# Sums of squares of the forget projections: eight fp32 products against sixteen products of rounded parts made by VectorE

## The reference, cut to what matters

```python
h = rms_norm(x, mix_norm[i])
fq, fk, fv, f_logit, sq, sk, sv, g_fox, g_sb = split_columns(h @ w_in[i])
fq = rms_norm(fq.reshape(b, s_len, FOX_HEADS, HEAD_DIM), q_norm[i])
fk = rms_norm(fk.reshape(b, s_len, FOX_HEADS, HEAD_DIM), k_norm[i])
log_f = jax.nn.log_sigmoid((f_logit + forget_bias[i]).astype(jnp.float32))
y_fox = forgetting_attention(fq, fk, fv, log_f)   # uses F = jnp.cumsum(log_f, axis=1)
```

## Time and profile before

| what | value |
| --- | --- |
| median of 3 runs | 1674.89 us (1674.73 to 1675.24) |
| the profiled execution | 1675.06 us, span 1673.3 us |
| TensorE busy | 1667.3 us (100%), 7640 matmuls |
| VectorE busy | 1029.0 us (61%) |
| ScalarE busy | 638.6 us (38%) |
| GpSimd busy | 713.3 us (43%) |
| granted clock of TensorE | 1.00 |

### The profile page before, as it was taken

How to read it: one execution, slowest core, us unless ns; L and a number is a source line. 1 busy time by engine, 2 the same in 40 slices (tenths; PEclk the granted TensorE clock), 3 DMA queues, 4 the chain that set the end, 5 groups by cost and what they waited for, 6 DMA issues and landing times.

```text
span 1673.3 us, 21109 instructions
## 1 busy us (share of the span) xinstructions
PE 1667.3 (100%) x7640; PEld 1363.7 (81%) x7640; DVE 1029.0 (61%) x1237; ACT 638.6 (38%) x895; POOL 713.3 (43%) x303
## 2 busy tenths in 40 slices
PE   9999999999999999999999999999999999999999
PEld 7887888887788887888888888888778768888887
DVE  7767566526565458367665567776574753969451
ACT  5222222226665756321322322213446744333321
POOL 2444344434333431444444344434356533444443
PEclk9999999999999999999999999999999999999999
DMA  5332232325511320342433323332252033323343
GB/s 199 101 110 90 81 101 93 107 90 197 139 64 53 99 76 26 101 138 90 141 97 103 103 88 100 103 103 89 93 193 76 26 124 104 95 94 101 94 142 117
DMA packets 44192, 173.14 MB, mean 103 GB/s; under 512 B 5033, under 2 KB 5417, under 8 KB 42828
## 3 DMA queue, kind: packets, MB, share of 16 engines
q1 hardware_dynamic: 39024, 148.13, 27.2%
q10 hardware_dynamic: 5084, 23.82, 4.2%
HBM read 159.22 MB, written 10.62 MB: 101 GB/s over the span
## 4 chain that ended last, share of the span: by engine, by line
PE 96%; DVE 2%; ACT 1%; issue 0%; DMA 0%; POOL 0%; SPq 0%; DVEq 0%; ACTq 0%; POOLq 0%
PE psum L339 26%; PE psum L340 26%; PE psum L344 26%; PE psum L1297 1%; PE psum L331 1%; PE psum L333 1%; PE psum L332 1%; PE psum L363 1%; PE psum L366 1%; PE psum L399 1%; PE psum L1883 1%; PE psum L400 1%; PE psum L404 1%; PE psum L369 1%; PE psum L1860 1%; PE psum L1287 1%
## 5 line engine op out<-in xcount | busy, mean ns | idle before, releaser
L274 POOL TENSOR_TENSOR wlo<-raw,whi 128x1024 fp32r<-128x1024 f32 (+2 forms) x256 | 657.9, 2570 | 866.5 <-ACT whi L319 865.9
L319 ACT ACTIVATE whi<-raw 128x1024 fp32r<-128x1024 f32 (+2 forms) x259 | 286.1, 1105 | 699.8 <-PE psum L344 633.8
L339 PE MATMUL psum<-h_hi,whi 128*128 128x512 f32 x1304 | 515.1, 395 | 0.1
L340 PE MATMUL psum<-h_lo,whi 128*128 128x512 f32 x1304 | 507.9, 389 | 0.0
L344 PE MATMUL psum<-h_hi,wlo 128*128 128x512 f32 x1304 | 324.4, 389 | 0.0
L339 PEld LDWEIGHTS psum<-h_hi,whi 128*128 128x128 f32 x1304 | 244.9, 188 | 55.2 <-issue 4.9
L340 PEld LDWEIGHTS psum<-h_lo,whi 128*128 128x128 f32 x1304 | 244.9, 188 | 52.3 <-issue 2.6
L344 PEld LDWEIGHTS psum<-h_hi,wlo 128*128 128x128 f32 x1304 | 244.8, 188 | 50.9
L725 DVE TENSOR_TENSOR silu<-sig,gate 128x512 f32<-128x512 f32 x44 | 100.3, 2279 | 41.8 <-ACT sig L670 41.8
L339 PE MATMUL psum<-mid_hi,whi 128*128 128x512 f32 x308 | 120.1, 390 | 0.0
L340 PE MATMUL psum<-mid_lo,whi 128*128 128x512 f32 x308 | 119.8, 389 | 0.0
(11 more groups left out here) (423 smaller groups left out, 2504.6 us busy)
## 6 DMA issues: line engine op xcount, KB each, us to landing
raw<-wk_dram SPq DMA_DIRECT2D x220, 512.0 KB, 3.5
raw<-wd_dram SPq DMA_DIRECT2D x32, 704.0 KB, 4.1
raw<-wp_dram SPq DMA_DIRECT2D x8, 640.0 KB, 3.8
x_scratch<-xT ACTq DMA_DIRECT2D x2, 2048.0 KB, 8.5
spectra_scratch<-spec_out ACTq DMA_DIRECT2D x4, 1024.0 KB, 6.4
xT<-x_scratch ACTq DMA_DIRECT2D x8, 512.0 KB, 4.5
spec<-spectra_scratch ACTq DMA_DIRECT2D x2, 2048.0 KB, 10.3
xT<-x_dram SPq DMA_DIRECT2D x4, 512.0 KB, 7.5
```

The source lines that it names most:

```text
L274: pool.tensor_tensor(wlo[s][:, 0:w], raw[s][:, 0:w], whi[s][:, 0:w].bitcast(F32), ALU.subtract).then_inc(lo_ready, 1)
L319: act.activation(whi[s][:, 0:w], raw[s][:, 0:w], ACT.Copy).then_inc(hi_ready, 1)
L339: pe.matmul(dst, a, m_hi[:, c, :], start=start and c == chunks[0][0], stop=False)
L340: pe.matmul(dst, a, m_lo[:, c, :], start=False, stop=False)
```

## The change

Three things change in `FoxProjections`, and two carry them.

1. **Parts of the squares.** ScalarE still writes the square in plain float32. VectorE now makes a rounded part `head_sq_hi` (a cast, L1154 of the changed kernel) and the rest `head_sq_lo` (a subtraction, L1156). TensorE multiplies both parts by a float32r copy of the matrix, `block_ones_r` (L1039, L1040), and sum j waits for both parts. The parts of unit j + 1 are made ahead of the scaling of i = j, those of units 0 and 1 ahead of the first scaling.
2. **The scan.** `vector_sums` stands behind i = 7 and no longer behind i = 4.
3. **The last factor.** ScalarE computes the factor of unit 7 directly after that of unit 6, ahead of the high parts of unit 6.
4. `block_ones_r` takes the place of a mask that nothing used in the constants, and the rotary tables count on the semaphore `const_landed`. Neither changes the number of DMAs or their place.

```diff
             def tensor_square_sum(self, pe, i):
-                pe.wait_ge(self.sq, i + 1)
+                pe.wait_ge(self.sq_parts, 2 * i + 2)
                 if i >= 2:
                     pe.wait_ge(self.std, i - 1)
-                pe.matmul(bank(4 + i % 2), block_ones, head_sq[i % 2][:, :], start=True, stop=True).then_inc(self.sum, 1)
+                pe.matmul(bank(4 + i % 2), block_ones_r, head_sq_hi[i % 2][:, :], start=True, stop=False)
+                pe.matmul(bank(4 + i % 2), block_ones_r, head_sq_lo[i % 2][:, :], start=False,
+                          stop=True).then_inc(self.sum, 1)
...
                         if j >= 2:
-                            act.wait_ge(self.sum, j - 1)
+                            act.wait_ge(self.sq_parts, 2 * j - 2)
                         act.activation(head_sq[j % 2][:, :], self.bank(j), ACT.Square).then_inc(self.sq, 1)
...
+                    if 0 < j < 8:
+                        i = j - 1
+                        self.scalar_factor(act, i)
+                        if j == 7:
+                            self.scalar_factor(act, 7)
...
+                self.vector_square_parts(dve, 0)
                 for i in range(8):
+                    if i + 1 < 8:
+                        self.vector_square_parts(dve, i + 1)
                     dve.wait_ge(self.rstd, i + 1)
...
                         self.vector_steps(dve)
-                    elif i == 4:
+                    elif i == 7:
                         self.vector_sums(dve)
...
+            def vector_square_parts(self, dve, j):
+                hi, lo = head_sq_hi[j % 2], head_sq_lo[j % 2]
+                dve.wait_ge(self.sq, j + 1)
+                if j >= 2:
+                    dve.wait_ge(self.sum, j - 1)
+                dve.tensor_copy(hi[:, :], head_sq[j % 2][:, :]).then_inc(self.sq_parts, 1)
+                dve.wait_ge(self.sq_parts, 2 * j + 1)
+                dve.tensor_tensor(lo[:, :], head_sq[j % 2][:, :], hi[:, :].bitcast(F32),
+                                  ALU.subtract).then_inc(self.sq_parts, 1)
```

More of the change, by code:

```diff
@@ L125, in build @@
         ident, block_ones, ones, before = (constf[:, i, :] for i in range(4))
-        ident_r, neg_tri, neg_ones, mask_qk, mask_kq = (constr[:, i, :] for i in range(5))
+        ident_r, neg_tri, neg_ones, mask_qk, block_ones_r = (constr[:, i, :] for i in range(5))
         head_sq = [square, sumsq]
@@ L160, in build @@
         forgets = at(100, "forgets", [P, T], F32R)
+        head_sq_hi = [at(88 + 2 * i, f"head_sq_hi{i}", [P, T], F32R) for i in range(2)]
+        head_sq_lo = [at(92 + 2 * i, f"head_sq_lo{i}", [P, T], F32R) for i in range(2)]
         probT = [at(104 + 2 * i, f"probT{i}", [P, T]) for i in range(2)]
@@ L413, in build @@
         const_landed = sem("const_landed")
-        rope_landed = sem("rope_landed")
         constr_ready = sem("constr_ready")
@@ L991, in __init__ @@
                 (self.sq, self.sum, self.std, self.rstd, self.f32, self.hi, self.ready, self.cleared, self.forget,
-                 self.softplus, self.v) = (
+                 self.softplus, self.v, self.sq_parts) = (
                     sem(f"fox_{x}") for x in ("square", "head_sum", "std", "rstd", "f32", "hi", "qk_ready", "constants",
-                                              "forget", "softplus", "v"))
+                                              "forget", "softplus", "v", "square_parts"))
             def unit(self, j):
@@ L1085, in scalar, with scalar_factor @@
                 split_hi_to(act, BASE["fox_v"] + 6)
+            def scalar_factor(self, act, i):
+                act.wait_ge(self.sum, i + 1)
+                if i == 7:
+                    act.wait_ge(self.rstd, i)
+                act.activation(std[:, :], bank(4 + i % 2), ACT.Ln, scale=1.0 / HD, bias=col("eps")).then_inc(self.std, 1)
+                act.wait_ge(self.std, i + 1)
+                if i:
+                    act.wait_ge(self.f32, i)
+                act.activation(rstd[:, :], std[:, :], ACT.Exp, scale=-0.5).then_inc(self.rstd, 1)
             def copy_again(self, act, keys):
@@ L1743, in load @@
             def load(self, act):
-                act.dma_start(rope[:, :], rope_in).then_inc(rope_landed, 16)
+                act.dma_start(rope[:, :], rope_in).then_inc(const_landed, 16)
                 for a, b, n in ((0, 96, 32), (32, 64, 32), (64, 0, 64)):
-                    act.dma_start(rope_odd[a:a + n, :], rope_in[b:b + n, :]).then_inc(rope_landed, 16)
+                    act.dma_start(rope_odd[a:a + n, :], rope_in[b:b + n, :]).then_inc(const_landed, 16)
             def tensor_latents(self, pe):
@@ L2129, in vector_latents @@
                 low, high = slice(HD, QKD), slice(QKD, P)
-                dve.wait_ge(rope_landed, 64)
+                dve.wait_ge(const_landed, 176)
                 dve.tensor_scalar(tab_q[:, :], rope[:, :], col("g_qn"), QKD ** -0.5, ALU.mult,
@@ L3183, in _constants @@
     mask_qk = np.where(i[None, :] > i[:, None], np.float32(NEG), np.float32(0))
-    mask_kq = np.where(i[:, None] >= i[None, :], np.float32(NEG), np.float32(0))
-    constr = np.stack([eye, tri, -np.ones((P, P), np.float32), mask_qk, mask_kq], 1)
+    constr = np.stack([eye, tri, -np.ones((P, P), np.float32), mask_qk, blocks], 1)
     pos = np.arange(T, dtype=np.float32)
```

## The result

| | before | after |
| --- | --- | --- |
| median | 1675.05 us (6 runs, 1674.73 to 1675.51) | 1682.44 us (6 runs, 1681.30 to 1683.82) |
| profiled execution, span | 1675.06 us, 1673.3 us | 1682.96 us, 1681.2 us |
| VectorE busy | 1029.0 us | 1043.6 us |
| mean granted clock of TensorE | 1.000 | 0.998 |

The ratio is 1.0043, with a 95% interval of 1.0034 to 1.0053. The changed kernel is slower by 7.4 us. I had forecast slower, by 5.0 us (1679.9), with a range that ended at 1682.0: the direction and most of the mechanism came out, the size did not.

A forecast was written before the change was run, and what follows sets the result against it. TensorE, 96% of the chain that ended last, was taken to bound the kernel. Waits of 8.9 us less 3.9 us gained gave +5.0 us, so 1674.89 + 5.0 = 1679.9 us, range 1675.0 to 1682.0.

The forecast's parts named there:

- sum 0 waits: At sum 0, TensorE waits 0.6 us for unit 0's parts, whose subtraction starts just ahead of GpSimd.
- weights of unit 3, sum 2: TensorE waits 0.1 us for ScalarE's delayed rounding for unit 3, and 0.2 us at sum 2 behind GpSimd.
- sum 3: The gates' logits stand ahead of unit 3's parts on VectorE: 1.8 us wait, 0.5 in the milder case.
- sum 5: Two ScalarE DMA issues ahead of the square and VectorE's `vector_steps` ahead of the cast: 1.1 us wait.
- sum 6: Sum 6 waits 1.45 us because ScalarE and VectorE stay late from round to round.
- sum 7: Due only 12 matmuls behind sum 6, its parts a whole late round behind: 3.6 us wait.
- gain: At TensorE's eight sums, cheaper products save 3.6 us and a vanished wait for ScalarE up to 0.3: 3.9 us.
- The late loop: At units 6 and 7, a late ScalarE lets GpSimd in ahead of the subtraction; rounds of 6.8 us stay late.
- The scan's move: The 1.2 us scan joins the chain to the first scores, which has 3.0 us to spare: cost 0.
- Hidden parts: Rival: VectorE's parts never meet GpSimd, 3.3 us of waits, -0.6 us, 1674.3; as before or partly hidden 0.20.
- free gain: Rival: no wait at any sum, -3.9 us, 1671.0; chance of all hidden and faster 0.06.
- slow cast: Rival: casts take 0.69 us, all subtractions from unit 2 on meet GpSimd, +9.1 us, 1684.0; over +6 us 0.09.

The follow-up runs named there:

- without parts: Changed kernel, but both products of a sum read one rounded square from ScalarE and VectorE makes no parts (sums inexact): 1671.85 us against 1675.12 before.
- filler: Changed kernel with 11 extra unused products on TensorE ahead of sum 0 and 13 ahead of sum 7: 1680.63 us against 1675.12 for the kernel before.
- second profile: The changed kernel timed and profiled again with no edit: 1682.36 us against 1675.10 for the kernel before.
- only the order changed: Kernel before with the scan and last factor moved, plus the change's semaphore and constants; squares and sums as before: 1674.93 us against 1675.09.
- gates' steps moved: Changed kernel with squares of units 2 to 6 in PSUM, sums 0 and 7 in float32, and the gates' steps behind i = 4: 1674.29 us against 1675.09 before.
- PSUM: Changed kernel with the squares of units 0 and 2 to 6 written to a PSUM bank instead of SBUF: 1677.81 us against 1675.12 for the kernel before.
- parts only: Changed kernel with the scan and the last factor back in their old places: 1683.49 us against 1675.09 for the kernel before.

## Why the prediction was wrong

By distances between sums, the forecast and the first profile compare so (the distance less the 5.89 us of a round without waits, 3.17 us for sums 6 to 7, and 19.5 us behind sum 7, which are the 20.25 of before less the sum's 0.45 and the factor's 0.3):

| step of the forecast | forecast | measured |
| --- | --- | --- |
| sum 0 waits | 0.6 | 2.7 |
| half clock behind sum 0 | - | 1.5 |
| weights of unit 3, sum 2 | 0.3 | 0.0 |
| sum 3 | 1.8 | 0.1 |
| sum 5 | 1.1 | 0.6 |
| sum 6 | 1.45 | 1.6 |
| sum 7 | 3.6 | 3.5 |
| half clock behind sum 7 | - | 1.7 |
| gain | -3.9 | -3.9 |
| total | +5.0 | +7.8 |

**What held.** A rounded pair costs 0.45 us instead of 0.90 (5.89 us apart, and -3.3 us without parts). The subtraction meets GpSimd and takes 2.7 to 2.8 us, and reading PSUM avoids that. The late loop closed at units 6 and 7: their squares lie at 437.89 and 444.60, 6.7 us apart, where I had worked out 6.8, and the waits at sums 6 and 7 are those of the forecast within 0.2 us. The scan's move was hidden, and the last factor gave its 0.3 us.

**Which step took it out of the range.** It was the missing term for the clock. With the clock held at 1.00 the same kernel, fillers and all, took 1680.63 us, +5.5 and inside the range; the changed kernel took 1682.44. That +5.5 lies so near to the forecast +5.0 is in part luck: the wait at sum 0 was priced 2.1 us too low, and those at sums 3 and 5 together 1.45 us too high (0.9 and 0.55 us in the filler's profile, 1.8 and 1.1 in the forecast).

**What failed, first: no term for the clock.** A pause of TensorE was priced at its length. At the pauses of 2.54 and 3.17 us came stretches at 0.50, together about 3 us in this profile (7.36 us behind sum 0 and 21.24 behind sum 7, where the filler kernel has 6.03 and 19.63). The filler shows the net price, 1.8 us, since most of the first stretch would have been waited at sum 3 anyway: the second profile, without it, has its first scores only 0.34 us sooner.

**What failed, second: the race at sum 0.** The forecast says "so the parts of unit 0 are ready at 401.3, the subtraction just ahead of GpSimd's 400.74: a wait of 0.6 us." I took GpSimd's start from the profile of before as fixed. It hangs on a DMA: ScalarE rounded those weights at 399.31 instead of 399.60, GpSimd started at 400.45, and the subtraction at 400.65 came second. I had treated such a race as open for unit 2 and as decided for unit 0, where the margin was as small as 0.1 us. It fell the same way in both profiles of the changed kernel, and in the six others in which VectorE's first pair reads SBUF: GpSimd was ahead by 0.20 to 0.33 us each time. Even with only the order changed, GpSimd started 0.18 us behind the small instruction of VectorE (400.51 and 400.33), against 0.72 us in the profile of before, so the profile that I forecast from had GpSimd later than any that I took afterwards with the same work on it. Priced by itself this term was 2.1 us too small.

**What failed, third, the other way.** The wait at sum 3 was 1.8 us in my layout and next to nothing in the first profile (0.7 in the second). It followed from the others: TensorE came 3.3 us later to it than laid out (422.67 instead of 419.4), the parts only 1.5 us later (422.59 instead of 421.1).

Hidden parts (1674.3) and a free gain (1671.0) are out, and so is the slow cast (1684.0): the casts took 0.36 to 0.43 us unless GpSimd was ahead. The range ended halfway to this last case; it should have held both outcomes of the race at sum 0, which alone moves its end by up to 2.1 us.

What stays open: why the 2.54 us pause at sum 0 brought the half clock in one execution and not in another. The 2.5 us spread of the first six executions goes with the clock: the slowest two have the lowest means (1683.82 at 0.997, 1682.96 at 0.998), the other four, 1681.30 to 1682.61, have 0.999. How much of it the clock makes isn't shown.

## What to carry to other kernels

Work that is given to VectorE must be priced against what GpSimd holds at that moment: an instruction of 0.7 us with two SBUF inputs was one of 2.7 us when GpSimd started 0.2 us earlier, and a row of before says when GpSimd started, not when it will. Look at the consumer with the shortest notice (here the first and the last of eight), leave these on the old path, and put the shared operand in PSUM if a bank is free; together this turned +7.4 us into -1.9. And a pause of TensorE of 2 to 3 us can cost more than its length.

## What the runs showed of the hardware that was not expected

- The length of a pause of TensorE alone did not say whether the half clock comes. It came with 1.94 us (the profile with the gates' steps moved), with 2.69 us, with 2.54 us in one profile of the changed kernel and with 3.17 and 3.19 us in both; it stayed away with 2.54 us in the other, with 2.74 us (PSUM) and with 3.20 us (parts only). At sum 0 of the changed kernel it fell before the pause was over, at sum 7 about 1.5 us after it, while TensorE was busy.
- With products that nobody reads run in the pauses, all six executions had a mean clock of 1.000, and the kernel was 1.8 us faster.
- A subtraction of VectorE that GpSimd kept out ended 0.55 us behind GpSimd's end (442.59 and 442.04 at unit 6). GpSimd, kept out by VectorE at unit 5, ended 2.25 us behind VectorE (437.30 and 435.05).
- GpSimd casts 128x512 elements in 0.61 us in most places, and took 1.08 us (396.79 in the kernel where it makes the parts) beside VectorE.
- ScalarE's two DMA issues ahead of the square of unit 5 took 1.37 or 1.38 us in every profile but one, and 3.12 us in that; the two at about 399.5 took 1.26 to 2.66 us.
